# Scaling the softmax inside the turning product: diagonals of the inverse sums in two self-attentions

## The reference, cut to what matters

```python
sc_own = einsum('bhtd,bhsd->bhts', q_c, k_own) * scale - slopes * dist
p = softmax(scores)                     # first block
out = einsum('bhts,bhsd->bhtd', p, v)
...
p_s = masked_softmax(s_s, dist_s >= 0)  # second block, selected and window branches
o_s = einsum('bgqhk,bgqkd->bqghd', p_s, v_g)
out = g[0] * o_c + g[1] * o_s + g[2] * o_w
```

## Time and profile before

| | value |
|---|---|
| median of three launches | 2286.92 us |
| profiled execution, span | 2288.81 us, 2286.9 us |
| first block's attention, first score to the next stage's first product | 119.6 to 159.1 us |
| second block's attention, the same | 1382.5 to 1544.3 us |
| TensorE busy, mean granted clock | 2164.6 us (95%), 0.97 |
| GpSimd busy | 328.7 us (14%) |
| share of TensorE in the chain that ended last | 87% |

### The profile page before, as it was taken

The page is one execution under the profiler, slowest core; times in us unless marked ns, Lnnn a source line. Parts: engine busy times, 40 slices in busy tenths (PEclk is TensorE's granted clock), DMA queues, the critical chain, the costliest instruction groups (busy, mean ns, idle before and its releaser), DMA issues.

```text
span 2286.9 us, 37526 instructions
## 1 busy us (share of the span) xinstructions
PE 2164.6 (95%) x16084; PEld 1665.3 (73%) x16084; DVE 1096.9 (48%) x1787; ACT 826.1 (36%) x1385; POOL 328.7 (14%) x407
## 2 busy tenths in 40 slices
PE   7989999999999899987999899998999889999999
PEld 5857888887666799972876565546779557888887
DVE  4255444445666444438234344555353445666532
ACT  3164423224355223234245135653323333222211
POOL 1441000003024100011000015651210011000000
PEclk9999999999999999997999899998999999999999
DMA  4112222232242100000353330003224102222222
GB/s 162 68 47 88 97 92 93 93 101 84 76 156 74 49 4 4 4 3 30 98 145 130 123 93 28 1 1 122 90 93 139 55 28 92 92 92 97 92 92 88
DMA packets 47845, 178.21 MB, mean 78 GB/s; under 512 B 5392, under 2 KB 5904, under 8 KB 46913
## 3 DMA queue, kind: packets, MB, share of 16 engines
q1 hardware_dynamic: 43488, 154.12, 20.2%
q0 software_dynamic: 4192, 21.70, 3.1%
HBM read 166.30 MB, written 10.55 MB: 77 GB/s over the span
## 4 chain that ended last, share of the span: by engine, by line
PE 87%; DVE 5%; ACT 4%; issue 2%; POOL 1%; DMA 0%; SPq 0%; DVEq 0%; ACTq 0%; POOLq 0%
PE ps L295 19%; PE ps L296 19%; PE ps L300 19%; PE ps L2304 9%; PE ps L781 4%; PE ps L1511 3%; PE ps L1259 2%; PE ps L2317 2%; PE ps L1243 1%; PE ps L770 1%; ACT arena L1354 1%; PE ps L1212 1%; DVE arena L1315 1%; PE ps L2672 1%; DVE arena L1299 1%
## 5 line engine op out<-in xcount | busy, mean ns | idle before, releaser
L275 ACT ACTIVATE w_hi<-wring 128x1024 fp32r<-128x1024 f32 (+1 forms) x243 | 254.2, 1046 | 572.4 <-PE ps L300 568.8
L281 DVE TENSOR_TENSOR w_lo<-wring,w_hi 128x1024 fp32r<-128x1024 f32 (+1 forms) x243 | 298.1, 1228 | 292.4 <-ACT w_hi L275 291.7
L2304 PE MATMUL ps<-arena 64*64 64x64 f32 x4096 | 135.7, 219 | 6.3 <-issue 5.5
L295 PE MATMUL ps<-ffn_input_hi,w_hi 128*128 128x512 f32 x352 | 139.5, 396 | 0.0
L296 PE MATMUL ps<-ffn_input_hi,w_lo 128*128 128x512 f32 x352 | 139.1, 395 | 0.0
L2304 PEld LDWEIGHTS ps<-arena 64*64 64x64 f32 x4096 | 130.2, 135 | 8.5 <-issue 7.0
L2404 ACT ACTIVATE arena<-ps 128x512 f32<-128x512 f32 x120 | 71.7, 597 | 178.3 <-PE ps L2304 178.3
L1401 POOL TENSOR_TENSOR arena<-arena 128x512 f32<-128x512 f32 (+3 forms) x160 | 111.4, 721 | 39.6 <-DVE arena L1307 34.6
L295 PE MATMUL ps<-mlp_input_hi,w_hi 128*128 128x512 f32 x256 | 101.6, 397 | 0.0
L295 PE MATMUL ps<-mlp_hi,w_hi 128*128 128x512 f32 x256 | 101.2, 395 | 0.0
L296 PE MATMUL ps<-mlp_input_hi,w_lo 128*128 128x512 f32 x256 | 101.2, 395 | 0.0
(11 more groups left out here) (407 smaller groups left out, 4433.3 us busy)
## 6 DMA issues: line engine op xcount, KB each, us to landing
wring<-weights SPq DMA_DIRECT2D x276, 512.0 KB, 3.3
bias_wide_scratch<-bias_line_scratch POOLq DMA_DIRECT2D x1, 4096.0 KB, 25.6
arena<-bias_wide_scratch POOLq DMA_DIRECT2D x1, 4096.0 KB, 17.1
wring<-weights SPq DMA_DIRECT2D x8, 384.0 KB, 3.0
arena<-x_t SPq DMA_DIRECT2D x4, 512.0 KB, 7.7
xn_scratch<-arena POOLq DMA_DIRECT2D x1, 2048.0 KB, 7.4
x_scratch<-arena POOLq DMA_DIRECT2D x1, 2048.0 KB, 8.3
arena<-xn_scratch POOLq DMA_DIRECT2D x1, 2048.0 KB, 8.8
```

What stands on the lines that cost most here:

```text
L275: act.activation(self.w_hi[:, m % SPLIT, 0:n], self.wring[:, g % RING, 0:n], ACT.Copy).then_inc(self.w_hi_ready, 1)
L281: dve.tensor_tensor(self.w_lo[:, m % SPLIT, 0:n], self.wring[:, g % RING, 0:n], self.w_hi[:, m % SPLIT, 0:n].bitcast(F32), ALU.subtract).t ...
L295: pe.matmul(out, hi[:, c, :], src.hi[:, at + c, :], start=(at + c == 0), stop=False)
L2304: mm = pe.matmul(cut(out, p, e), cut(lhs, p, e), right, start=(i == 0), stop=(i == len(terms) - 1))
```

## The change

GpSimd no longer multiplies `p`. For each i it forms one 128 x 256 tile in `k.square`: for each head the identity with its ones replaced by the row's inverse sum (times the gate, where there is one). The blocks are turned by a plain float32 product of the block of `p` (stationary) with that diagonal (moving) in place of the transpose with the identity; the product turns the block and scales it. Everything else, the order of TensorE's work too, stays. The wait before a part is now one for both heads.

```diff
+    def diagonal(self, u, i):
+        return self.k.square[:, 2 * (u % 2) + i // 2, (i % 2) * 2 * P:(i % 2 + 1) * 2 * P].rearrange("p (e t) -> p e t", e=2)
...
     def probs_t(self, pe, u, part):
-        ident = self.k.const("ident")
+        pe.wait_ge(self.scaled, NT * u + NT - part)
         for e in range(2):
             p = self.b.p[u % 2][e]
-            pe.wait_ge(self.scaled, 8 * u + 2 * (NT - 1 - part) + e + 1)
...
-                    mm = pe.transpose(out[:, at:at + P], p[:, TRI[i] + j * P:TRI[i] + (j + 1) * P], ident)
+                    mm = pe.matmul(out[:, at:at + P], p[:, TRI[i] + j * P:TRI[i] + (j + 1) * P],
+                                   self.diagonal(u, i)[:, e, :], start=True, stop=True)
...
-                for e in range(2):
-                    seg = b.p[u % 2][e][:, TRI[i]:TRI[i] + P * (i + 1)]
-                    pool.tensor_tensor(seg, seg, inv[:, e:e + 1].to_broadcast([P, P * (i + 1)]), ALU.mult).then_inc(
-                        self.scaled, 1)
+                ident = self.k.const("ident").unsqueeze(1).to_broadcast([P, 2, P])
+                pool.tensor_tensor(self.diagonal(u, i), ident, inv.unsqueeze(2).to_broadcast([P, 2, P]), ALU.mult).then_inc(
+                    self.scaled, 1)
```

## The result

The changed kernel takes 2320.85 us (median of 4 executions, 2318.98 to 2323.31) against 2286.76 (4 executions of the kernel before, 2285.74 to 2288.31): 34.1 us more, ratio 1.0142, 95% interval 1.0130 to 1.0154. The forecast was 2312, range 2303 to 2322. The profiled execution took 2318.98 us with a span of 2317.1, which is 30.2 us over the span before.

The account below looks back on a forecast made before the run. TensorE, busy 95% of the span, was taken to set the pace. First block +6.1 and second +22.2 make +28.3 us, less 3.2 for the clock is +25.1; on the median 2286.9 that gives 2312, range 2303 to 2322.

Parts of the forecast that it names:

- TensorE sets the pace, GpSimd is hidden: In both attentions: TensorE sets the pace and GpSimd's scaling is nearly all hidden; its relief saves 0.8 us once.
- Two records of 0.1116 us: Turned block at line 1243: its product is two records, 0.223 us, 0.102 more than a transpose; 2.04 us a unit.
- 0.65 us of waits covered: Per unit: TensorE's waits of 0.29 (VectorE's bias row) and 0.36 (ScalarE's copy) vanish, so 2.04 us costs 1.41.
- the third wait: Behind the last turned block, before scores i = 2: TensorE's wait for VectorE's move and bias stays, 0.42 or so.
- Units of 10.26, 10.84 and 11.27: Unit lengths after the change: 10.26 us in the first block, 10.84 and 11.27 in the second, +1.41 each.
- The ends: Last unit of each attention +1.88 us; second block's first unit +0.6, as 0.8 of its 1.41 is saved.
- the 6.1 of the sum: First block's attention at an unchanged clock: 3 x 1.41 + 1.88 = 6.1 us more.
- The low clock gone: Second block's attention end: TensorE's low-clock stretch disappears, -3.2 us; the rival that it stays or moves: 2315, chance 0.22.
- The Trainium skill's factor of four: Turned block: a product costs four transposes, 0.36 us more for each of 400 blocks; rival at 2419, chance 0.01.
- From the profiled run to the median: Whole kernel: the median lies 1.9 us below the profiled run's 2288.81, so 2313.9 becomes 2312.

Follow-up runs that it names:

- The product alone: Kernel before, each block turned by a plain float32 product with the identity, GpSimd still scaling the probabilities: 2323.11 us against 2291.6.
- e2: Changed kernel with transposes with the identity back; GpSimd forms the diagonals but nothing uses their values: ratio 0.9957 to the kernel before.
- e7_twice: Changed kernel with every product issued twice into the same place: 2413.61 us (one execution).
- e5_three_moves: e4_copy_first plus head 0 of part 0 ahead of scores i = 0, output copy behind the bias of i = 0: 2276.36 us against 2288.36.
- e4_copy_first: Kernel before with ScalarE's copy of head 0's part 1 ahead of the exps of i = 2: 2282.45 us against 2288.36.
- e3_half: Kernel before with the product with the identity for head 0 and the transpose for head 1: 2297.32 us against 2291.6.
- e11_after_moves: Changed kernel with the three edits of order of e5_three_moves: 2324.85 us against 2288.55 for the kernel before.
- e9_one_record: Changed kernel with probabilities and diagonals in fp32r, so a product is one record: 2292.72 us against 2288.36 for the kernel before.
- e12_early_ends: e5_three_moves with VectorE's output copy back in its old place in the last two steps: 2272.99 us against 2288.55 for the kernel before.
- e10_one_record_moves: e9_one_record with the three edits of order of e5_three_moves: 2279.18 us against 2288.36 for the kernel before.

## Why the prediction was right, and where it was short

- *TensorE sets the pace, GpSimd is hidden:* right. The product alone makes the 10.53 us unit; GpSimd's relief alone is worth 0.07 us a unit and 1.0 at the second block's start, 2 us. How e2's untraced executions came to 6 us and more below is open.
- *Two records of 0.1116 us:* right as a pace (0.112 in e7_twice, 12 records in 1.34 us). The step from it to 0.102 us more for each block was short. I took the transposes' pace in a group of six, 0.12, but that 0.12 holds something that is paid once: from the first transpose of a group to the second it is 0.17, from each other to the next 0.11. Groups of 6, 8 and 10 transposes take 0.80, 1.02 and 1.24 (e5_three_moves, e4_copy_first), that is 0.11 each and 0.14 once. Products cost 0.223 each and 0.20 once. So a block costs 0.113 more, and each of the three groups 0.06 more, which my sum didn't have: 20 x 0.113 + 3 x 0.06 = 2.44. The groups as measured (1.54, 1.54 and 1.98 against 0.81, 0.81 and e4's 1.02) grew by 2.42, against my 2.04. That is the mis-sized term: 0.38 a unit.
- *0.65 us of waits covered, the third wait kept:* right in kind. e3_half shows them covered once, e5_three_moves and e11_after_moves show that it is the same idle time, and the eight scores kept their 2.11. The size was 0.73, since a group cut in two by the wait pays its 0.14 twice: I had read part 0 without its wait as 0.55 + 0.55, and it is 1.02. Of the 0.38 above, 0.08 went there.
- *Units of 10.26, 10.84 and 11.27:* measured 10.53, 11.11 and 11.53. Over 17 units the miss of 0.27 is 4.6 us, nearly all of the gap between my +25.1 and the +30.2 of the two spans.
- *The ends:* 1.88 more from the last blocks to the last values, and in the first block 165.00 - 159.39 = 5.61 against 3.73 is just that. The 1.2 us by which this block grew beyond the 6.1 of the sum is three units at 0.27 and 0.4 at its start and first unit. The first unit of the second block cost 11.53 against 10.70 (from 1388.97), +0.8 for my +0.6.
- *The low clock gone:* the values and their compressed part took 3.31 us (1566.18 - 1562.87), as forecast. The rule of the Trainium skill on transpose mode (TensorE: Matmul & The Clock Gate, PE-mode transpose), which I had behind it, is not borne out as the reason. The clock is low there with no transpose in the stage in e9_one_record, twice, and in part in e11_after_moves (values 3.57); with transposes it is full in e5_three_moves and e12_early_ends (values 2.37). And in the kernel before it is also low at 124.8 to 127.7 us, granted 0.54, in scores ahead of the stage's first turned block. What decides it is open: e5_three_moves has full clock behind a wait of 1.87 us, e10_one_record_moves 4.54 us values behind one of 1.86. So that the 3.2 us came back in the traced execution is shown; that they came back because of the products isn't. The term was luck, and it mattered: 3.2 us more in every execution would put the median at 2324, outside the range.
- *The Trainium skill's factor of four* (TensorE: Matmul & The Clock Gate, Terms) is 2 in this kernel: 0.22 us for a product, 0.11 for a transpose. The trace disagrees with it, as line 781 had said.
- *From the profiled run to the median:* the profiled execution of before was 2.0 us above the median of 2286.76, that of after 1.9 below its own. Those 3.9 us are the rest of the 34.1.

## What to carry to other kernels

Before moving work from an idle engine into an instruction of the busiest one, count that instruction's records: a float32 product that also scales is two records where a transpose is one. Read the waits of the pacing engine first. Here the same waits that hid three tenths of the new cost were worth some 10 us to a mere change of order. And measure a half dose too: whether cost is proportional tells what was covered. Last, look whether a low clock comes or goes in the trace before giving a total to the edit: here it was 3.2 us of several totals.

## What the runs showed of the hardware that was not expected

- A one-record (fp32r) product of a 128 x 128 block with 128 moving columns costs TensorE what a float32 transpose does (six in 0.89 us against 0.88), and scales on the way. It didn't pay here, since nothing waited for GpSimd.
- A group of float32 products costs some 0.2 us once beside 0.112 us for each record (12 records 1.54, 24 records 2.88, 32 records 3.77 us from start to next start). It stands at both ends of the group: the first record to the second takes 0.21 us for 0.11, the last to the first score 0.20. Transposes cost 0.11 us each and 0.14 once (0.17 and 0.20 at the ends). What causes it was not tested.
- GpSimd multiplies two broadcast operands into 128 x 256 in 614 ns, exactly the mean of a 128 x 256 instruction with one broadcast column.
